# A hybrid trunk layer on one core: expert weights in 4 KB packets, gathers that skip padding, and four changes of order

## The reference

```python
h = rms_norm(x, norm_mix)
proj = h @ w_in                       # 1024 -> 7.4 k columns
o_a = forgetting_attention(fq, fk, fv, ff + fox_f_bias, ...)   # 8 heads of 64
log_a = log_sigmoid(glr @ gla_w_lr + gla_b_gate) / 16.0
o_b = gla_chunked(gq, gk, gv, log_a)                           # 4 heads, chunks of 64
o_b = rms_norm(o_b, gla_out_norm) * silu(gr)
o_c = mamba2_branch(sz, sxbc, sdt, ...)                        # SSD, 8 heads, chunks of 64
gates = sigmoid(gate_pre + b_branch_gate)
x = x + sum(gates * (branches @ w_branch)) @ w_out
t = rms_norm(x, norm_ffn)
# top-1 of 4 groups, then top-2 of that group's 4 experts
for e in range(16):
    hid = silu(t @ w_exp_gate[e]) * (t @ w_exp_up[e])          # 1024 -> 512
    out = out + combine[:, e:e + 1] * (hid @ w_exp_down[e])    # 512 -> 1024
x = x + out
```

## Time and profile before

| | us |
|---|---|
| median of 3 runs | 920.07 |
| the profiled execution | 920.09 |
| its span in the profile | 917.7 |
| PE busy | 843.7 (92%) |
| DVE busy | 574.4 (63%) |
| ACT busy | 466.7 (51%) |
| POOL busy | 110.1 (12%) |
| first expert item starts on PE | 603.7 |
| last scatter is issued | 906.7 |

### The profile page before, as it was taken

How to read it: one execution, slowest core, us unless ns; L and a number is a source line. 1 busy time by engine, 2 the same in 40 slices (tenths; PEclk the granted TensorE clock), 3 DMA queues, 4 the chain that set the end, 5 groups by cost and what they waited for, 6 DMA issues and landing times.

```text
span 917.7 us, 11182 instructions
## 1 busy us (share of the span) xinstructions
PE 843.7 (92%) x4072; PEld 668.1 (73%) x4072; DVE 574.4 (63%) x641; ACT 466.7 (51%) x543; POOL 110.1 (12%) x107
## 2 busy tenths in 40 slices
PE   2999999999999899999999998279999999989983
PEld 2667776777877678888888885168888888867762
DVE  5646438862745876324533517649899889877880
ACT  5454535463445352321322313057887888777860
POOL 5310000000000110100000100012232223222100
PEclk9999999999999899999999999679999999999996
DMA  6421112212112112222326584859999999999981
GB/s 196 145 89 50 46 60 80 92 47 92 47 46 92 38 55 92 92 92 92 96 94 217 172 302 165 309 184 322 374 371 351 376 371 364 362 372 371 370 270 24
DMA packets 85177, 169.38 MB, mean 185 GB/s; under 512 B 8761, under 2 KB 9874, under 8 KB 85138
## 3 DMA queue, kind: packets, MB, share of 16 engines
q1 hardware_dynamic: 76080, 145.89, 45.0%
q0 software_dynamic: 4896, 17.83, 7.4%
q10 hardware_dynamic: 4162, 5.13, 1.7%
HBM read 155.21 MB, written 13.63 MB: 184 GB/s over the span
## 4 chain that ended last, share of the span: by engine, by line
PE 56%; DMA 27%; DVE 9%; ACT 3%; issue 3%; SPq 0%; POOL 0%; DVEq 0%; ACTq 0%; POOLq 0%
PE bank L1763 16%; PE bank L1765 15%; PE bank L1764 15%; DMA mstage<-in_w_exp_down 10%; DMA mstage<-in_w_exp_up 9%; DMA mstage<-in_w_exp_gate 7%; PE bank L1874 1%; DVE stt L1410 1%; PE bank L1905 1%; PE bank L2084 1%; PE bank L1890 1%; ACT whi L673 1%; DVE wlo L686 1%; PE bank L1862 1%; PE bank L2006 1%
## 5 line engine op out<-in xcount | busy, mean ns | idle before, releaser
L686 DVE TENSOR_TENSOR wlo<-mstage,whi 128x2048 fp32r<-128x2048 f32 x96 | 218.6, 2291 | 42.0 <-ACT whi L673 41.3
L673 ACT ACTIVATE whi<-mstage 128x2048 fp32r<-128x2048 f32 x96 | 184.0, 1918 | 49.6 <-PE bank L1765 31.9
L686 DVE TENSOR_TENSOR wlo<-stage,whi 128x2048 fp32r<-128x2048 f32 (+1 forms) x40 | 90.8, 2273 | 107.1 <-ACT whi L673 106.6
L1763 PE MATMUL bank<-hTh,whi 128*128 128x512 f32 x368 | 149.5, 406 | 0.0
L1765 PE MATMUL bank<-hTh,wlo 128*128 128x512 f32 x368 | 144.0, 391 | 0.0
L1764 PE MATMUL bank<-hTl,whi 128*128 128x512 f32 x368 | 143.8, 391 | 0.0
L673 ACT ACTIVATE whi<-stage 128x2048 fp32r<-128x2048 f32 (+1 forms) x40 | 74.9, 1873 | 80.6 <-PE bank L1765 74.8
L1763 PE MATMUL bank<-whi,xTh 128*128 128x512 f32 x256 | 104.1, 406 | 1.9 <-DVE xTl L1705 1.8
L1765 PE MATMUL bank<-whi,xTl 128*128 128x512 f32 x256 | 101.0, 394 | 0.0
L1764 PE MATMUL bank<-wlo,xTh 128*128 128x512 f32 x256 | 100.8, 394 | 0.0
L1763 PEld LDWEIGHTS bank<-hTh,whi 128*128 128x128 f32 x368 | 69.5, 189 | 16.5 <-issue 2.8
(11 more groups left out here) (366 smaller groups left out, 1298.2 us busy)
## 6 DMA issues: line engine op xcount, KB each, us to landing
mstage<-in_w_exp_gate SPq DMA_DIRECT2D x32, 1024.0 KB, 11.7
mstage<-in_w_exp_up SPq DMA_DIRECT2D x32, 1024.0 KB, 13.9
mstage<-in_w_exp_down SPq DMA_DIRECT2D x32, 1024.0 KB, 12.3
stage<-in_w_in SPq DMA_DIRECT2D x28, 1024.0 KB, 5.0
stage<-in_w_branch SPq DMA_DIRECT2D x6, 1024.0 KB, 5.0
stage<-in_w_out SPq DMA_DIRECT2D x4, 1024.0 KB, 5.0
xin<-in_x SPq DMA_DIRECT2D x4, 512.0 KB, 5.5
x<-in_x SPq DMA_DIRECT2D x4, 512.0 KB, 7.3
```

The lines of the kernel that those rows point to most:

```text
L673: nc.scalar.activation(whi[:, s, :, 0:n], source_of(u)[:, :, 0:n], ACT.Copy).then_inc(hi_ready, 1)
L686: nc.vector.tensor_tensor(wlo[:, s, :, 0:n], source_of(u)[:, :, 0:n], whi[:, s, :, 0:n].bitcast(F32), ALU.subtract).then_inc(lo_ready, 1)
L1763: t.matmul(out, lhs[0], rhs[0], start=start, stop=False)
```

## The change

**Weights in 4 KB rows.** A unit of gate or up weights is now laid out so that partition p holds weight rows 2p and 2p+1 of each group of 256, so that one packet carries two rows that lie side by side in DRAM; a unit of down weights is 256 whole rows of 1024 columns in place of 512 half rows. A unit stays 1 MB; it is 256 packets of 4 KB in place of 512 of 2 KB.

```diff
-                sp.dma_start(mstage[k][:, :, :], src).then_inc(mstaged[k], 16)
+                sp.dma_start(mstage[k][:, :, :].rearrange("p (g r) n -> p g (r n)", r=2), src).then_inc(mstaged[k], 16)
...
-                    return w[e, kh * 512:(kh + 1) * 512, :].rearrange("(j p) n -> p j n", p=P)
+                    return w[e, kh * 512:(kh + 1) * 512, :].rearrange("(g p r) n -> p g (r n)", p=P, r=2)
...
-                    return w_exp_down[e, :, nh * 512:(nh + 1) * 512].rearrange("(j p) n -> p j n", p=P)
+                    return w_exp_down[e, fh * 256:(fh + 1) * 256, :].rearrange("(j p) n -> p j n", p=P)
```

```diff
-                        k = 4 * half + q
-                        ins = t.transpose(bank[b][:, q * P:(q + 1) * P], xg[:, par, k * P:(k + 1) * P], ident[:, :])
+                        c = 512 * half + 256 * (q // 2) + q % 2
+                        ins = t.transpose(bank[b][:, q * P:(q + 1) * P], xg[:, par, c:c + 255:2], ident[:, :])
...
-                    ins = expert_unit(u + nh, whole(2 + nh), (hdh, hdl), True, True, m=m, per=uper)
-                    ins.then_inc(full[2 + nh], 1)
+                for fh in range(2):
+                    su = (u + fh) % RING
+                    pe.wait_ge(lo_ready, after(m, uper, u + fh + 1))
+                    for j in range(2):
+                        for nh in range(2):
+                            f, c = 2 * fh + j, 2 * j + nh
+                            ins = passes(whole(2 + nh), (hdh[:, f, :], hdl[:, f, :]),
+                                         (whi[:, su, c, :], wlo[:, su, c, :]), f == 0, f == 3)
+                            if f == 3:
+                                ins.then_inc(full[2 + nh], 1)
+                    if fh == 0:
+                        ins.then_inc(unit_used, 1)
```

```diff
-        h2d = nc.dram_tensor("h2rows", [T + P, D], F32).ap()
+        h2d = nc.dram_tensor("h2rows", [T, D], F32).ap()
...
-                                     bass.IndirectOffsetOnAxis(tabid[:, i:i + 1], 0)).then_inc(xg_in[par], 16)
+                                     bass.IndirectOffsetOnAxis(tabid[:, i:i + 1], 0), bounds_check=T - 1,
+                                     oob_is_err=False).then_inc(xg_in[par], 16)
```

```diff
-    out = [("small",)]
-    early = {(0, 0, 1): [("loga",)], (0, 0, 2): [("lo", 2)], (0, 0, 3): [("logs",)], (1, 0, 3): [("tokrows",)],
-             (1, 1, 0): [("bcum",)]}
+    out = [("smalls",)]
+    early = {(0, 0, 1): [("small",)], (0, 0, 2): [("lo", 2)], (0, 0, 3): [("loga",)], (0, 1, 1): [("logs",)],
+             (1, 0, 3): [("tokrows",)], (1, 1, 0): [("bcum",)]}
```

```diff
-        out += los + squash
...
         out += [("hi", 2 * p[1] + p[2] + 2) for p in taken if p[3] == 0 and p[4] == 0]
+        out += los
+        if not los and convs < 6 and ("piece", 3 + convs // 4, 1, convs % 4, 1) in rest[:max(done - 1, 0)]:
+            out += [("conv", convs), ("squash", convs)]
+            convs += 1
```

More of the change, by code:

```diff
@@ L655, in wait_unit @@
                 i = NEXP + w
-                which, n = ((unit_used, NB + 9 + 2 * i), (full[0], B0[0] + i + 1), (unit_used, NB + 10 + 2 * i),
-                            (full[1], B0[1] + i + 1), (full[2], B0[2] + i + 1), (full[3], B0[3] + i + 1))[k]
+                first = NB + 9 + 3 * i
+                which, n = ((unit_used, first), (full[0], B0[0] + i + 1), (unit_used, first + 1),
+                            (full[1], B0[1] + i + 1), (unit_used, first + 2), (full[3], B0[3] + i + 1))[k]
             items = 1 if ovf else 2
-            eng.wait_ge(which, after(m, 2 * items if which is unit_used else items, n))
+            eng.wait_ge(which, after(m, 3 * items if which is unit_used else items, n))
         def split_hi(act, u, m=None, ovf=False):
@@ L804, in _ @@
             step(g.tensor_tensor(rst[:, :], ssq[:, :], mhalf[:, 0:NT], ALU.pow), rst_done, 1)
+            pool.wait_ge(wsmh_done, 1)
+            step(g.tensor_tensor(wsml[:, :, :], wsm[:, :, :], wsmh[:, :, :].bitcast(F32), ALU.subtract), wsml_done, 1)
             step(g.memset(reset16[:, :], 1.0))
@@ L878, in _ @@
             step(g.memset(zero[:, :], 0.0))
-            g.dma_start(h2d[T:T + P, :], zero[:, :]).then_inc(pad_out, 16)
             g.dma_start(acc[T:T + P, :], zero[:, :]).then_inc(pad_out, 16)
@@ L947, in _ @@
             a.activation(wsmh[:, :, :], wsm[:, :, :], ACT.Copy).then_inc(wsmh_done, 1)
+            act.wait_ge(rst_done, 1)
+            for i in (2, 3):
+                a.activation(xn[:, i, :], xin[:, i, :], ACT.Copy, scale=rst[:, i:i + 1]).then_inc(xna_done, 1)
             split_hi(act, 0)
-            split_hi(act, 1)
             act.wait_ge(cols_done, 1)
@@ L1098, in _ @@
                     step(a.activation(oraw[:, h % 2, :], whole(b), ACT.Copy))
-                    step(a.activation(osq[h % 2][:, :], whole(b), ACT.Square), free[b], turn(b, ("go", h)) + 1)
+                    step(a.activation(osq[h][:, :], whole(b), ACT.Square), free[b], turn(b, ("go", h)) + 1)
                 elif kind == "gout":
@@ L1180, in _ @@
             act.wait_ge(acc_in, 16 * NT)
-            act.wait_ge(pad_out, 32)
+            act.wait_ge(pad_out, 16)
             def x_hi(n, par, m=None, per=2):
@@ L1273, in _ @@
                                             ssq[:, i:i + 1]), ssq_dve, i + 1)
-            dve.wait_ge(rst_done, 1)
-            for i in range(NT):
-                dve.wait_ge(x_in[i], 16)
-                step(v.tensor_scalar(xn[:, i, :], xin[:, i, :], rst[:, i:i + 1], None, ALU.mult), xn_done, i + 1)
             dve.wait_ge(full[0], 1)
@@ L1283, in _ @@
             step(v.tensor_scalar(gain1[:, 1:2], cols[:, R_FQ:R_FQ + 1], -FOX_HD ** -0.5, None, ALU.mult), cols_done, 1)
-            dve.wait_ge(wsmh_done, 1)
-            step(v.tensor_tensor(wsml[:, :, :], wsm[:, :, :], wsmh[:, :, :].bitcast(F32), ALU.subtract), wsml_done, 1)
+            dve.wait_ge(rst_done, 1)
+            for i in range(2):
+                step(v.tensor_scalar(xn[:, i, :], xin[:, i, :], rst[:, i:i + 1], None, ALU.mult), xn_done, i + 1)
             split_lo(dve, 0)
-            split_lo(dve, 1)
             for n, k in enumerate(KORDER):
@@ L1787, in _ @@
                     take(0, "hT")
-                for i in range(NT):
+                t.transpose(bank[k][:, 0:P], xn[:, 0, k * P:(k + 1) * P], ident[:, :])
+            pe.wait_ge(xn_done, 2)
+            pe.wait_ge(xna_done, 2)
+            for k in KORDER:
+                for i in range(1, NT):
                     ins = t.transpose(bank[k][:, i * P:(i + 1) * P], xn[:, i, k * P:(k + 1) * P], ident[:, :])
@@ L1793, in _ @@
                 kind = it[0]
-                if kind == "small":
+                if kind in ("smalls", "small"):
                     pe.wait_ge(wsml_done, 1)
-                    for k in KORDER:
+                    for k in KORDER[:5] if kind == "smalls" else KORDER[5:]:
                         pe.wait_ge(free[k], turn(k, "hT") + 1)
@@ L1799, in _ @@
                                      k == KORDER[0], k == KORDER[-1])
-                    ins.then_inc(full[4], 1)
+                    if kind == "small":
+                        ins.then_inc(full[4], 1)
                 elif kind == "loga":
```

47 lines of the change are left out of this document (22 added, 25 removed).

## The result

The changed kernel takes 906.26 us in the median (904.44 to 909.45, 4 runs) against 918.77 us for the kernel before (917.11 to 920.16, 4 runs): ratio 0.9868, 95% interval 0.9833 to 0.9904, so 12 us faster, and inside the forecast range of 891 to 911. The forecast itself, 899.6, was 6.7 us too low. The profiled execution of the changed kernel took 904.44 us, the fastest of its four, with a span of 902.6 us; its profile is set against that of before, 917.7.

The account below looks back on a forecast made before the run. PE bounds most of the kernel but for a few holes; queue q1 bounds the expert phase from about 800 us. Terms -8.4 - 2.8 - 0.5 - 3.2 - 2.6 - 3.0 = -20.5 give 899.6 us, range 891 to 911.

Parts of the forecast that it names:

- The skipped gathers first: Expert supply on q0: half the row places are padding, so 64 packets of 222 ns go, 0.9 us an item.
- the step that took 174 ns for a 4 KB packet: Expert weights on q1: a 4 KB packet costs two old ones of 86.9 ns, so no gain from size.
- the addition of shares: Expert supply: q1's and q0's packet times added over 16 engines, 20.2 us an item, near the 19.9 seen.
- The beat: Expert phase: scatters stay 17.72 us apart up to the last but one, 879.6 in place of 888.05, -8.4 us.
- ACT's order: Expert items: up split ahead of the first `yrow` starts 0.7 us sooner, both rows fit behind; cost 0, margin nearly nothing.
- Rival A: Expert items: both `yrow` wait for bank 3, ACT is 0.7 us later, PE waits 0.65 an item: 908.7 us; chance 0.12.
- The last period: End of the expert phase: split units lie ready, only PE's own chain is left, 15.9 us, -2.8.
- First gather: Path into the expert phase: the first gather has half its packets, -0.5 us.
- First phase, attention and SSD: Before the experts: PE's old waits go or shrink, new ones at second square and second block; -3.2, -2.6, -3.0 us.
- rival C: First half gives nothing, each hole filled opens another of its size: 908.4 us; chance 0.10.
- signs of being right: Among them: scatters 17.7 us apart, q1 below 90 ns per 2 KB, DMA share under 1 late in the expert phase.
- B: Expert supply stays at 19.9 us, skipped rows still take queue time; the phase only ends better: 911 us; chance 0.10.

Follow-up runs that it names:

- s4: The kernel before with the second of three matmuls left out of every expert product, plus 4 KB weight packets and skipped padding: period 18.95 us.
- s1: The kernel before with the second of three matmuls left out of every expert product, 2 KB packets, padding gathered: period 19.90 us, 914.85 us in all.
- s2: The kernel before with the second of three matmuls left out of every expert product, 2 KB packets, padding skipped by the gathers: period 19.84 us.
- e1: The kernel before with only the gathers' edit (`bounds_check`, no zero rows), weights still in 2 KB packets: 917.62 us, ratio 0.9985.
- t4: The changed kernel with `logs` and the second `gmul` moved later and h2's even and odd columns stored apart: 902.54 us, ratio 0.9814.
- t3: The changed kernel with ACT's old order back, first `yrow` ahead of the split of unit u + 5: 931.15 us, ratio 1.0127.
- t2: The changed kernel with the second `gmul` behind `ssdA` 1 and the low split one block later: 904.38 us, ratio 0.9830.
- t1: The changed kernel with `logs` moved ahead of block 1: 904.59 us, ratio 0.9849.

## Why the prediction was right, and where it was not

**The bound.** Right: from 650 us PE and the transfers compete, the store of buffers hides the difference for ten items, and the change takes the late periods away. The supply after the change was put at 19.0 us an item; s4 measures 18.95. That this number came out is luck, as it has the wrong reason. The step that failed is "The skipped gathers first: half of the row places are padding, so 64 packets of 222 ns go, 0.9 us an item": the packets do not go (1008 more of under 512 B), and what they save is 0.05 us of the period (s1 against s2, 19.90 and 19.84), 0.2 by e1. And the step that took 174 ns for a 4 KB packet left out 9.4 ns, 0.90 us an item. The two errors cancelled. Had only the gathers been changed, the same reasoning would have forecast 9 to 11 us where 1.2 came.

What misled was the addition of shares. q0's share fell in e1 from 7.4% to 6.3%, 10 us an engine, or some 0.5 us an item without the removed zero rows, yet the period moved far less. The shares of all queues together give 1.05 of an engine's time, so the times of some packets overlap, and the price of one of them is not what the period would lose without it. Whether the rest of a skipped row's price lies in the queue or in the memory was not tried.

**The rule.** The Trainium skill, "DMA: Bandwidth & Descriptors", section "Why small descriptors are slow (HBM only)", made the step from 2 to 4 KB worth some 2% of the weights' time, an estimate of 0.4 us an item. The runs show 0.90, 5.4% of a packet's price: the direction agrees, the measured size is over twice the page's and decides. The page's "only worth it at ≤256 B desc size" is on joining descriptors, and was no guide for the longer rows of this kernel, whose bound they moved.

**The beat.** 17.72 was taken for the changed kernel, 17.85 came: -7.0 in place of -8.4. Of the 0.13 us, some 0.07 is the strided weight load that t4 takes away; the other 0.06 is open. The prediction took no extra for it, with the Trainium skill's page "SBUF — State Buffer", whose cachelines make strides up to four fp32 values free. PE's weight load does not follow it: 205 against 140 ns. The bound of twice the time, 1.0 us an item, was too wide: of the 0.52 us that the loads take longer, most lies beside other matmuls.

**ACT's order.** "Cost 0, but the margin is nearly nothing" was right, and t3 shows how right: without the new order the margin is -1.7 us an item. Rival A did not happen.

**The last period.** -2.8 was forecast, -1.7 came: PE's waits for `hid` and `hdl` shrank only by 0.4 us, to 2.29 and 1.41, and the lower clock stayed (0.79 in the window from 878 to 886 us, below).

**First gather.** -0.5 forecast, nothing seen: PE waited 5.65 us for it, 5.66 before. By the sum's reasoning that is the same error, the price of a padded row.

**First phase, attention and SSD.** The mechanisms were right, down to the new wait at the second square (2.5 forecast, 2.66 seen) and the one for the second block. That one was forecast at 1.2 to 2.6 us and is 3.03, which the prediction had named as a sign of being wrong (over 3 us), and the lower clock that was to go with the old waits follows it in part; rival C came true for a third of the SSD's part. In attention both waits for `prob` went, for 2.1 of the 2.6 us.

**The other signs.** Of the signs of being right one did not come: the DMA share stayed at 1.03 in the window from 800 to 850 us and not under 1. The supply, 18.95 us an item, is still slower than PE's 17.85; what changed is that the store outlasts a difference of 1.1 us. The sum says the same (19.0 against 17.72), so this sign contradicted it.

**A rival's sum.** B says that the phase "ends better", but its 9.3 us leave out the 2.8 of the last period; with them it is 908.0 and not 911. The upper end of the range came from it, and the measured 906.26 lies under either.

**The medians.** The median lies 1.8 us above the profiled execution and the slowest 5.0. Only the fastest has a trace, but one cause can be seen: the granted clock after short waits. The wait for the second square (2.66 us at 54.7 us, and 2.67 in t2) leaves the clock at 1.00 in the profiled execution of the changed kernel, and in that of t2 it falls to 0.50, the lower of the two levels:

```profile
55.00:61.00 6.00, 6.00 (x24) 4.27 (x23) 2.54 (x3) 4.76 (x6) 2.39 (x2) 1.00 0.01 3
```

```profile
55.00:61.00 6.00, 5.83 (x12) 3.96 (x13) 1.88 (x4) 4.57 (x6) 2.49 (x2) 0.50 0.00 1
```

t2's first scores start at 101.25 us, 3.3 later than the changed kernel's; 0.45 of that is older than the wait. The four executions of the changed kernel had mean clocks of 0.974, 0.972, 0.972 and 0.968 in the order of their times, which fits. The times of t4, without that wait, lie within 2.0 us, those of t1, also without it, within 2.6, those of t2, with it, within 3.7. The lower level remains at the end, where the waits for `hid` and `hdl` stand; the changed kernel and t4:

```profile
878.00:886.00 8.00, 4.30 (x14) 3.08 (x13) 3.26 (x3) 0.60 (x1) 0.00 (x0) 0.79 0.27 53
```

```profile
878.00:886.00 8.00, 6.73 (x17) 5.29 (x18) 0.69 (x1) 0.49 (x1) 0.00 (x0) 0.57 0.01 2
```

So a wait that was moved, not removed, costs its length in each execution and can cost some 3 us more in some of them, as in t2's. The prediction gave this a place in the range, but no term in the sum.

## What to carry to other kernels

Before counting on a saving in one queue, run the transfers as the bound (leave out compute until they are) and read the period with and without it: runs of that kind would have put both prices right here. When a product is reordered so that its results come later, look at what is queued behind their reader on its engine; one instruction in the old place cost more than the change brought. And count a new wait on PE with the clock that may fall behind it.

## What the runs showed of the hardware

A 4 KB packet on q1 costs 164 ns against 86.9 for 2 KB by the periods (159 to 164 by q1's share), in a stream that holds 358 to 389 GB/s. Indices that a gather skips stay as packets of under 512 B (1008 of 1024) and give back 0.05 to 0.2 us of a period of 19.90 for 64 of them. A transposition's weight load with every second fp32 column takes 205 ns in place of 140. After a wait of PE of 2.66 to 2.67 us at the same place of the program its granted clock was at its upper level in one execution and at the lower one in another.
